# A two-block transformer kernel with its planned instruction order set anew in every stage

## The reference, cut to what matters

```python
# first block
proj = xn @ w_in[l]
attn = _windowed_gqa(q_a, k_a, v_a, band_bias, in_window, attn_sink[l])
gdn = _gdn_mixer(qkv_g, z_g, a_g, b_g, conv_w[l], gdn_a_log[l], gdn_dt_bias[l], gdn_norm_w[l])
h = h + jnp.concatenate([attn, gdn], axis=-1) @ w_out[l]
h = h + jnp.square(jax.nn.relu(hn @ w_ffn_in[l])) @ w_ffn_out[l]
# second block, stick-breaking attention, per block of 128 queries
log_keep = jnp.where(mask, jax.nn.log_sigmoid(-logits), 0.0)
later = lax.cumsum(log_keep, axis=3, reverse=True) - log_keep
weights = jnp.where(mask, jnp.exp(jax.nn.log_sigmoid(logits) + later), 0.0)
out = jnp.einsum('bhqk,bkhd->bqhd', weights, vf)
# and its end
merged = jnp.sum(gates * proj, axis=2)
return x + rms_norm(jnp.einsum('bsd,de->bse', merged, w_out), g_post)
```

## Time and profile before

| | us |
|---|---|
| median of three runs (lowest, highest) | 2294.95 (2293.42, 2296.1) |
| span of the profiled execution | 2291.9 |
| PE busy in it | 2247.2 (98%) |
| DVE busy | 1594.7 (70%) |
| ACT busy | 1112.9 (49%) |
| POOL busy | 1030.9 (45%) |
| share of PE in the chain that ended last | 84% |

### The profile page before, as it was taken

How to read it: one execution, slowest core, us unless ns; L and a number is a source line. 1 busy time by engine, 2 the same in 40 slices (tenths; PEclk the granted TensorE clock), 3 DMA queues, 4 the chain that set the end, 5 groups by cost and what they waited for, 6 DMA issues and landing times.

```text
span 2291.9 us, 31262 instructions
## 1 busy us (share of the span) xinstructions
PE 2247.2 (98%) x11389; PEld 1785.5 (78%) x11389; DVE 1594.7 (70%) x2217; ACT 1112.9 (49%) x2008; POOL 1030.9 (45%) x643
## 2 busy tenths in 40 slices
PE   9999989999999999999999999999999999999999
PEld 6778867677878888887887777777777888888886
DVE  7865768776596554689449798888888655545745
ACT  5554157674364555444446365645433322225553
POOL 2212245444247666657767211111123765556663
PEclk9999999999999999999999999999999999999999
DMA  4113353344325443955452301111123343338554
GB/s 160 40 44 99 122 177 107 98 139 158 109 93 188 161 152 133 314 173 166 143 170 83 124 29 46 47 46 47 56 79 124 134 143 111 111 133 294 183 171 147
DMA packets 153764, 289.43 MB, mean 126 GB/s; under 512 B 34915, under 2 KB 44387, under 8 KB 153612
## 3 DMA queue, kind: packets, MB, share of 16 engines
q1 hardware_dynamic: 153612, 287.44, 38.3%
HBM read 207.88 MB, written 79.51 MB: 125 GB/s over the span
## 4 chain that ended last, share of the span: by engine, by line
PE 84%; DVE 8%; ACT 2%; issue 2%; DMA 2%; POOL 1%; SPq 0%; DVEq 0%; POOLq 0%; ACTq 0%
PE bank L869 12%; PE bank L871 12%; PE bank L867 12%; PE bank L639 12%; PE bank L643 11%; PE bank L641 11%; PE bank L716 2%; PE bank L932 2%; PE bank L963 1%; PE bank L945 1%; ACT t L1005 1%; DVE t L1434 1%; DVE t L1974 1%; PE bank L836 1%; PE bank L854 1%
## 5 line engine op out<-in xcount | busy, mean ns | idle before, releaser
L2100 POOL TENSOR_TENSOR t<-t,t 128x512 fp32r<-128x512 f32 (+1 forms) x494 | 810.5, 1652 | 1068.3 <-ACT t L1005 1062.1
L1005 ACT ACTIVATE t<-t 128x512 fp32r<-128x512 f32 (+1 forms) x689 | 448.3, 676 | 653.5 <-PE bank L871 276.3
L639 PE MATMUL bank<-t,t 128*128 128x512 f32 x1360 | 548.5, 403 | 0.0
L643 PE MATMUL bank<-t,t 128*128 128x512 f32 x1360 | 531.4, 391 | 1.1 <-DVE t L1434 0.6
L641 PE MATMUL bank<-t,t 128*128 128x512 f32 x1360 | 530.1, 390 | 1.7 <-POOL t L2100 1.7
L867 PE MATMUL bank<-t,t 128*128 128x512 f32 x1316 | 514.2, 391 | 6.2 <-DVE t L1818 4.6
L869 PE MATMUL bank<-t,t 128*128 128x512 f32 x1316 | 513.3, 390 | 1.4 <-POOL t L2100 1.4
L871 PE MATMUL bank<-t,t 128*128 128x512 f32 x1316 | 513.1, 390 | 0.7 <-DVE t L1434 0.7
L639 PEld LDWEIGHTS bank<-t,t 128*128 128x128 f32 x1360 | 255.7, 188 | 62.7 <-issue 12.7
L643 PEld LDWEIGHTS bank<-t,t 128*128 128x128 f32 x1360 | 255.3, 188 | 58.3 <-POOL t L2100 1.3
L641 PEld LDWEIGHTS bank<-t,t 128*128 128x128 f32 x1360 | 255.9, 188 | 56.3 <-issue 4.6
(11 more groups left out here) (250 smaller groups left out, 2641.2 us busy)
## 6 DMA issues: line engine op xcount, KB each, us to landing
t<-in_w SPq DMA_DIRECT2D x87, 512.0 KB, 3.6
hid_scr<-t SPq DMA_DIRECT2D x112, 256.0 KB, 2.1
t<-hid_scr SPq DMA_DIRECT2D x112, 256.0 KB, 2.7
t<-in_wf SPq DMA_DIRECT2D x80, 256.0 KB, 3.3
t<-in_wf SPq DMA_DIRECT2D x36, 512.0 KB, 4.5
g_scr<-t SPq DMA_DIRECT2D x36, 512.0 KB, 2.9
t<-g_scr SPq DMA_DIRECT2D x72, 256.0 KB, 3.4
t<-in_wo SPq DMA_DIRECT2D x24, 512.0 KB, 3.6
```

The costliest lines, as they stand in the source:

```text
L639: e.matmul(ps[:, :], hi[:, w, :], XH[:, x, hs], start=k == 0, stop=False)
L643: last = e.matmul(ps[:, :], hi[:, w, :], XL[:, x, hs], start=False, stop=k == j.nk - 1)
L1005: return e.activation(out, in_, ACT.Copy, **kw)
L2100: return e.tensor_tensor(out, x, high.bitcast(F32), ALU.subtract)
```

## The change

`SHIFT` is replaced by another table, with 78 entries where there were 55. The instructions stay the same, apart from two waits. In the step `ss` the last operation waits for all `st` groups of the piece two before, where it waited for the last one alone. And `sv` is given the previous `sv` as a step that must stand ahead of it on PE.

```diff
-SHIFT = {("abias",): 1.5, ("apv", 1): 1.25, ("atr", 3): -1.5, ("bg", 1): -1, ("bm2", 0): -0.25, ("bm2", 1): 3, ("cR", 1): 1.75, ("co", 0, 4): -2,
...
+SHIFT = {("abias",): 1, ("am", 0, 0, 2): 2.25, ("apv", 1): 0.5, ("aq", 0): 3.5, ("aqk", 5, 3): 1, ("atr",): -2, ("bel", 0): -1, ("bel", 0, 2): 1.75,
...
+         ("tx", 2): -4, ("tx", 3): -8, ("wc", 1, 9): 1.75, ("whi", 25): 9.25, ("wload", 1): -2.5, ("x", 2): -2, ("x1l", 1): 2.5, ("x2h",): 8,
...
-            q.wait_ge(done("st", i0, PIECES[p0][0], (PIECES[p0][2] - 1) // 256))
+            q.wait_ge(*[done("st", i0, PIECES[p0][0], g) for g in range(PIECES[p0][1] // 256, (PIECES[p0][2] + 255) // 256)])
...
-            add("pe", "sv", i, p_, rank=3)
+            add("pe", "sv", i, p_, rank=3, behind=[("sv", K.piece_before(12 * i + p_, 1))] if i or p_ else ())
```

More of the change, by code:

```diff
@@ L40 @@
 SCORE_RANK = {7: -0.5}
-SHIFT = {("abias",): 1.5, ("apv", 1): 1.25, ("atr", 3): -1.5, ("bg", 1): -1, ("bm2", 0): -0.25, ("bm2", 1): 3, ("cR", 1): 1.75, ("co", 0, 4): -2,
[6 rows of a table removed]
+SHIFT = {("abias",): 1, ("am", 0, 0, 2): 2.25, ("apv", 1): 0.5, ("aq", 0): 3.5, ("aqk", 5, 3): 1, ("atr",): -2, ("bel", 0): -1, ("bel", 0, 2): 1.75,
[4 rows of a table added]
+         ("smin", 0): 2.75, ("smin", 1, 2): -0.75, ("smin", 0, 2, 7): -1, ("smin", 0, 3, 7): 0.75, ("smin", 1, 1, 2): -5, ("smin", 1, 1, 8): -2,
[5 rows of a table added]
 PIECES = [(qb, 0, 128 * qb + 128) for qb in range(4)] + [(qb, *k) for qb in range(4, 8) for k in ((512, 128 * qb + 128), (0, 512))]
```

## The result

The changed kernel takes 2317.74 us (median of four runs, 2316.34 to 2320.32) where the old one takes 2294.77 in the same session: a ratio of 1.0099, 95% interval 1.0085 to 1.0114. It is 23 us slower. The forecast was 5 us faster, and the range ended at 2299.

What follows compares the result with a forecast made beforehand. PE bounds the kernel (busy 2247.2 of 2291.9 us; only 44.7 idle plus low-clock cost to regain). Terms A to H sum to -5.3 us on the median, forecast 2289.6, range 2280 to 2299.

Steps and rivals of the forecast that it cites:

- A: Start: second product at 12.2 instead of 8.33, part won back, 1.0 taken for clock; +2.4 us, bounds 0 to +5.
- B: 306 to 320: a wait on the `aq(0)` load replaces the wait on ACT before `lb`; 0 us, bounds -3.4 to +1.
- C: 320 to 530, GDN part: idle 2.90 before `cR(1,5)` goes once `as1(5)` stands behind `cs(1,4)`; -3.5 us, bounds -8 to +3.
- D: 527 to 537: `gg` moves behind four `yal`, so the awaited `yal` is done earlier; -1.2 us, bounds -1.5 to +0.5.
- E: 620 to 661: `fsum(1)` moved ahead of `fa(0,0)`, DVE earlier, no idle before `fa(0,1)`; -2.8 us, bounds -4.5 to +1.
- F: At 1214: `n2(0)` runs ahead of `n1(0)` and fills half of its 1.5 wait for POOL; -0.7 us.
- G: Stick-breaking, 1260 to 1770: the two new waits cost 0, moved steps gain or delay; +0.5 us, bounds -2 to +6.
- H: Last stage: no step that PE waits for moves; 0 us.
- Rival 2: The start decides, slower: A is +4.8 us; where C to G give nothing, 2299.8 us; chance 0.18.
- Rival 1: The many moves cancel, no change: sum -0.2 us, 2294.8; chance 0.2 together with another no-change rival.

Runs made afterwards that it cites:

- e8_aq: The old kernel with only the load of the queries `aq(0)` at its new rank: ratio 1.0004 to the old kernel.
- e7_as1: The old kernel with one DVE step moved, `as1(5)` behind `cs(1,4)` instead of ahead of `cO(1,4)`: ratio 0.9996 to the old kernel.
- e5_fsum: The old kernel with one PE step moved, the sum over features ahead of the first feed-forward product: ratio 1.0012 to the old kernel.
- four mixed tables: Four kernels, each with new ranks in one stage and old ones elsewhere: start 1.0019, GDN part 1.0037, feed-forward 1.0044, stick-breaking 1.0016, against the old kernel.
- e10_w1: The old kernel with one new start rank alone, the second weight tile loaded first: ratio 1.0009 to the old kernel.
- e11_waits: The changed kernel with the old table of ranks, leaving only the new waits of `ss` and `sv`: ratio 0.9997 to the old kernel.
- e12_gn: The changed kernel with one DVE step moved, `gn(0,4)` behind `cO(1,4)` and `cs(1,4)`: ratio 1.0099 to the old kernel.

## Why the prediction was wrong, by its own steps

**A, the start (+2.4; measured +3.8 at 306).** The mechanism and the time of the second product (12.2; 12.27) were right. The term that was mis-sized is the clock, 1.0 taken where eleven matmuls at 1.2 GHz cost 2.3. It is inside the bound of +5. (At 20 us the trace is 5.0 late. "Nothing takes the delay up" was not quite so: 1.2 come back, 0.8 of it at 39, where the old kernel waits 0.54 for DVE.)

**B, 306 to 320 (0; measured +0.7).** The sum of the four waits is 7.64 against 7.77, and L840 waits for the load from `qa_scr`, as the step had it. But the clock was low for 10.2 us instead of 6.8, as in `e8_aq`, and by 345 the changed kernel had lost another 3.1 us: 1.7 of the 3.8 since 306 are the clock and 2.0 are idle, with waits of 1.02 and 1.92 for DVE where the old trace has one of 1.23. What failed is "0": it counted idle time and left out what several idle times close to each other do to the clock behind them.

**C, the GDN part (-3.5; the stage lost 7.7).** This is the step that failed worst. It took 2.5 us as the price of `as1(5)`. The same step for the next block, from DVE's timeline of the old trace, where POOL is idle:

```profile
490.51 0.15 DVE L1636 TENSOR_TENSOR t<-t,t 128x8 f32<-128x8 f32 x1
490.69 0.17 DVE L1638 TENSOR_SCALAR t<-t 128x8 f32<-128x8 f32 x1
490.77 0.16 DVE L1639 TENSOR_TENSOR t<-t,t 128x8 f32<-128x8 f32 x1
```

At 447.9, with POOL running all the time (the old trace has its L2119 from 446.15 to 450.31 and L2140 behind it), the first two took 1.23 and 1.18. The 2.5 us were DVE's wait beside POOL:

```profile
449.17 1.18 DVE L1638 TENSOR_SCALAR t<-t 128x8 f32<-128x8 f32 x1
...
446.15 4.16 POOL L2119 TENSOR_TENSOR t<-t,t 128x512 f32<-128x512 f32 x3 [0.63 <-DVE t L1545]
```

The slow ones end with POOL's instructions, to 0.04 us: DVE's at 449.13 and 450.35, two of POOL's at 449.11 and 450.31. In `e7_as1` all three do (DVE 451.17, 452.40, 453.61; POOL 451.14, 452.37, 453.58). What stands there pays for it: `as1(5)` in its new place in `e7_as1` took 3.3, `gn(0,4)` takes 3.23, against 0.75 for the same operation at 488.3, where POOL is idle. The Trainium skill ("SBUF — State Buffer", Who interferes with whom) says that a DVE instruction with two inputs in SBUF, the on-chip memory of the tiles, and a GpSimd (POOL) instruction that reads SBUF exclude each other for a whole instruction, whichever starts first; the trace agrees for L1636, with 0.15 alone against 1.23 us. L1638 reads one tile only and was held as long. And "I have no row for the new ones", said of the shuffled small waits, was centred at zero; the traces of the new order show 1 to 4 us more of idle there and 4 us and more of PE's own time, most of it at the lower clock. The signs set down for this step told it: PE idle from the projection to `w_out` is 25.2 us, where it was to be below 18, and new waits of 2.8 and 3.55 us stand in it.

**D (-1.2; measured 0.0).** The 0.55 before the product is gone, and the 2.51 for ACT in front became 3.03. I had priced DVE's shift, where the wait was ACT's. And "PE ran at the low level here" was read wrongly: the clock was low from 531.7 to 535.1, and the product in question runs at 536.87.

**E (-2.8; measured +0.9 by `fa(1,1)`, +4.1 by the end of the feed-forward part).** Two sentences failed. "Its last input is ready at 626.3" used DVE's old order; the new one puts two low parts ahead, one of them beside POOL, and the input came 1.6 later. "`fr(1)` and DVE run up to 1.3 to 1.6 earlier": `e5_fsum` shows that `fr(1)` stands on ACT behind results of products that moved back, so DVE came later with the old order too; in the new order, where it doesn't, 11 slow operations instead of 8 made it 3.4 later. Behind `fa(1,1)` another 3.2 us are lost: 1.5 are idle at 684 and 698 (for DVE and for POOL), and of the rest no run shows the cause.

**F (-0.7; +2.9 with what follows it to 1273).** With the feed-forward ranks alone PE gained 0.8 at `n1` and `n2` and lost 1.1 behind them. In the changed kernel `n2(1)` waits 1.77 for DVE at 1274. None of the four mixed tables loses more than 0.3 us here, so it takes ranks of two stages together; which is open.

**G (+0.5; +2.9)** lies inside its bounds of -2 to +6, and the waits cost 0 as stated. Of the 2.9, 1.7 are idle (the longest waits are now 1.42 for DVE and 1.26 for ACT, 0.87 and 0.55 before) and 1.2 PE busy longer at the full clock. PE idle in the stage is 6.7, over the 5 that were to show a gap. **H (0; +2.1).** The first product of the last stage waits 0.81, as before, and the second 1.22 for POOL, 0.79 before: 0.4 to 0.5 us. Then the clock falls, which costs 1.6. It fell there in three of the twelve traces with the old order at this place (`e8_aq`, `e10_w1`, `e11_waits`, with the same idle times of 0.81 and 0.80 as the others) and in three of the five with the new one. So whether these 1.6 us come is partly chance, and whether the new order makes them more likely is not shown.

**The rivals.** Rival 2 (slower) had the right sign and its place gave the first 3.8 us, but it priced the start alone. (It says that 4.8 is under 60% of 7.7; it is 62%.) Rival 1 had the right mechanism, "a wait that goes leaves PE waiting for the same late engine a few steps on", as `e7_as1` and `e12_gn` show, but took it to end at no change. No rival put the GDN and feed-forward parts on the slower side, though the bounds of C (+3) and E (+1) reached there, and the 7.7 lost between 306 and 533 lie beyond C's bound even without B's 0.7. That is the flaw behind the range: every known wait was followed to its end, and every unknown one counted as zero.

## What to carry to other kernels

A wait that ends on a full queue does not go away with the instruction that stands last in it: four single moves (`as1`, `gn`, `hac`, `tx`) each shortened the wait they were aimed at by 0.8 to 3.2 us, and none gained anything that could be measured. Before an instruction's duration is counted as a saving, look at the same instruction elsewhere in the trace; if it is short there, the time belongs to the neighbour. And a reshuffled stretch without rows of its own should not be priced as zero: in this one case each of the four stages lost, the GDN part 7.7 us in 226.

## What was not expected of the hardware

The same three 128x8 operations of DVE took 0.48 us in one place and 2.6 in another, by whether POOL was running. In the 17 traces of this case they took over 0.7 us 60 times, and each time ended within 0.06 us of the end of a POOL instruction. TensorE's clock fell at the same place in some executions and not in others, behind the same two idle times of 0.81 and 0.80 us: 1.00 around 1773 in the old kernel's trace, 0.81 over 9 us in that of `e8_aq`. And behind the projection the place of the idle times counts, not their sum. In the eleven traces with the old place of the queries' load (7.7 to 8.0 us of idle in four waits, the last of about 5) the clock is low for 6.8 us, once for 3.4. In the six with the new place (6.3 to 8.3 us of idle) it is low for 10.2 in each, in one piece or in two.
